# Block inverse of the delta rule: where the second orientation of the inverse comes from in levels 0 to 4

## The reference

```python
decay = jnp.exp(jnp.where(tril, gc[..., :, None] - gc[..., None, :], -jnp.inf))
a_mat = jnp.where(strict, jnp.einsum('bhncd,bhnsd->bhncs', kb, kc) * decay, 0.0)
rhs = jnp.concatenate([vb, kb * jnp.exp(gc)[..., None]], axis=-1)
sol = lax.linalg.triangular_solve(a_mat, rhs, left_side=True, lower=True, unit_diagonal=True)
...
v_new = u_c - jnp.einsum('bhcd,bhde->bhce', w_c, state)
```

## Time and profile before

| | |
|---|---|
| runs (3) | median 1034.73 us, 1033.13 to 1035.6 |
| profiled execution | 1033.16 us, its span 1031.4 us |
| mean granted TensorE clock | 0.939 of full speed |
| busy: PE, DVE, ACT | 859.6, 347.2, 216.8 us |
| the inverse in layer 0 | from about 95 to 144 us of the span |
| the inverse in layer 1 | from about 607 to 655 us |

### The profile page before, as it was taken

The page is one execution under the profiler, slowest core; times in us unless marked ns, Lnnn a source line. Parts: engine busy times, 40 slices in busy tenths (PEclk is TensorE's granted clock), DMA queues, the critical chain, the costliest instruction groups (busy, mean ns, idle before and its releaser), DMA issues.

```text
span 1031.4 us, 18112 instructions
## 1 busy us (share of the span) xinstructions
PE 859.6 (83%) x6932; PEld 617.0 (60%) x6933; DVE 347.2 (34%) x773; ACT 216.8 (21%) x410; POOL 23.0 (2%) x26
## 2 busy tenths in 40 slices
PE   4999999989588867698679999999896877879665
PEld 3877887968354433444358778879674544445332
DVE  1656634424621111111126565344346111111112
ACT  1243222222311100011103442133123111111111
POOL 1000000000300000000000000000003000000000
PEclk9999999989899888899879999999998998989888
DMA  9913012534459999979955120134344799899993
GB/s 343 350 57 103 1 42 82 167 119 163 169 244 419 421 420 421 421 323 421 403 207 183 42 82 1 45 119 163 107 172 157 306 420 421 337 423 419 420 421 138
DMA packets 48474, 249.42 MB, mean 242 GB/s; under 512 B 6096, under 2 KB 18560, under 8 KB 19344
## 3 DMA queue, kind: packets, MB, share of 16 engines
q1 hardware_dynamic: 47824, 246.91, 60.4%
q0 software_dynamic: 576, 1.43, 0.5%
HBM read 247.50 MB, written 1.05 MB: 241 GB/s over the span
## 4 chain that ended last, share of the span: by engine, by line
PE 50%; DMA 23%; DVE 12%; issue 7%; PEld 2%; ACT 2%; PEldq 1%; SPq 1%; DVEq 1%; POOLq 0%; ACTq 0%
PE ps L477 16%; DMA ring<-e_down 15%; PE ps L784 5%; PE ps L912 5%; PE ps L942 5%; DMA ring<-e_up 4%; PE ps L492 3%; PE ps L881 3%; DMA shared<-e_down 3%; DVE kq L1425 3%; DVE shared L1430 2%; PE ps L685 1%; PEld ps L912 1%; PE ps L639 1%; PE ps L953 1%
## 5 line engine op out<-in xcount | busy, mean ns | idle before, releaser
L477 PE MATMUL ps<-hT,ring 128*128 128x256 f32 x864 | 191.0, 381 | 0.0
L477 PEld LDWEIGHTS ps<-hT,ring 128*128 128x128 f32 x864 | 162.7, 190 | 25.9 <-issue 2.5
L912 PE MATMUL ps<-ring,hT 128*32 128x256 f32 x1728 | 114.7, 424 | 43.0 <-DMA ring<-e_up 21.7
L912 PEld LDWEIGHTS ps<-ring,hT 128*32 128x32 f32 x1728 | 67.2, 122 | 90.6 <-issue 69.8
L881 PEld LDWEIGHTS ps<-kq 128*128 128x128 bf16 x960 | 65.0, 149 | 10.0 <-issue 7.4
L953 PE MATMUL ps<-hT,kq 128*128 128x512 f32 x144 | 66.1, 602 | 5.5 <-PE ps L942 5.5
L881 PE MATMUL ps<-kq 128*128 128x128 bf16 x960 | 67.9, 235 | 2.3 <-DVE kq L1608 2.3
L1608 DVE TENSOR_TENSOR kq<-shapes,sel 128x128 bf16<-128x128 f32 (+1 forms) x40 | 9.9, 288 | 156.0 <-PE ps L920 155.7
L942 PE MATMUL ps<-ring,kq 128*32 128x512 f32 x448 | 51.0, 595 | 13.1 <-DMA ring<-e_down 8.4
L784 PE MATMUL ps<-ring,xn 128*128 128x256 f32 x256 | 58.8, 385 | 0.0
L912 PE MATMUL ps<-shared,hT 128*32 128x256 f32 x576 | 39.8, 437 | 21.9 <-DMA shared<-e_up 20.4
(11 more groups left out here) (303 smaller groups left out, 976.9 us busy)
## 6 DMA issues: line engine op xcount, KB each, us to landing
ring<-e_gate SPq DMA_DIRECT2D x48, 1024.0 KB, 21.8
ring<-e_up SPq DMA_DIRECT2D x48, 1024.0 KB, 10.8
ring<-e_down SPq DMA_DIRECT2D x48, 1024.0 KB, 23.6
ring<-w_mix SPq DMA_DIRECT2D x34, 1024.0 KB, 10.1
shared<-e_down SPq DMA_DIRECT2D x16, 1024.0 KB, 7.8
shared<-e_gate SPq DMA_DIRECT2D x16, 1024.0 KB, 18.7
shared<-e_up SPq DMA_DIRECT2D x16, 1024.0 KB, 26.5
ring<-w_mix SPq DMA_DIRECT2D x12, 512.0 KB, 7.2
```

Of the source, the lines that this page charges most:

```text
L477: mm = pe.matmul(bank[:, ct * T:(ct + 1) * T], w[:, k, ct * P:(ct + 1) * P], hT3[:, k, :], start=(k == 0), stop=(k == KD - 1))
L912: mm = pe.matmul(ps[32 * e:32 * e + 32, 5 + m, 0:DE], hq[:, k, 32 * e:32 * e + 32], slot[at[e]][:, k * DE:(k + 1) * DE], start=(k == 0), s ...
```

## The change

In levels 0 to 4 the non-zero blocks of XT are at most 32x32 and lie on the diagonal, so a transpose of each 32x32 block in its place is the transpose of the whole matrix. The changed kernel makes X so, with one VectorE instruction per group on 128x512 elements, from SBUF to SBUF. The TensorE transposes and the ScalarE copies stay for level 5 only. The SiLU on three gate tiles (L1076) now comes right after `gates(4)`, and 15 entries leave the list of banks.

```diff
-    order += [("A", g) for g in range(3)] + [("gate", 4)] + [("X", 0, g) for g in range(3)]
+    order += [("A", g) for g in range(3)] + [("gate", 4)]
     for lev in range(1, 7):
         order += [("W", lev, g) for g in range(3)] + [("Z", lev, g) for g in range(3)]
-        if lev < 6:
+        if lev == 5:
             order += [("X", lev, g) for g in range(3)]
...
-                for g in range(3):
-                    bank = begin(("X", 0, g))
-                    pe.wait_ge(xt_ready, g + 1)
-                    for m in range(4):
-                        mm = pe.transpose(bank[:, m * P:(m + 1) * P], XT[:, 4 * g + m, :], c("ident"))
-                    done(mm, ("X", 0, g))
...
-                    if lev < 6:
+                    if lev == 5:
                         for g in range(3):
                             bank = begin(("X", lev, g))
...
-                for lev in range(6):
-                    for g in range(3):
-                        bank = get(("X", lev, g))
-                        link(act.activation(X[:, 4 * g:4 * g + 4, :], bank[:, :], ACT.Copy))
-                        act.sem_inc(x_ready, 1)
-                        act.sem_inc(free[bank_of[("X", lev, g)][0]], 1)
-                    if lev == 0:
-                        act.activation(mixT[:, 2:5, :], mixT[:, 2:5, :], ACT.Silu).then_inc(gate_ready, 1)
+                act.activation(mixT[:, 2:5, :], mixT[:, 2:5, :], ACT.Silu).then_inc(gate_ready, 1)
+                for g in range(3):
+                    bank = get(("X", 5, g))
+                    link(act.activation(X[:, 4 * g:4 * g + 4, :], bank[:, :], ACT.Copy))
+                    act.sem_inc(x_ready, 1)
+                    act.sem_inc(free[bank_of[("X", 5, g)][0]], 1)
...
                     dve.sem_inc(xt_ready, 1)
+                    link(dve.transpose(X[:, 4 * g:4 * g + 4, :], XT[:, 4 * g:4 * g + 4, :]))
+                    dve.sem_inc(x_ready, 1)
...
                         free_(("Z", lev, g))
+                        if lev < 5:
+                            link(dve.transpose(X[:, 4 * g:4 * g + 4, :], XT[:, 4 * g:4 * g + 4, :]))
+                            dve.sem_inc(x_ready, 1)
```

## The result

The changed kernel takes 1041.37 us (median of 12 runs, 1037.3 to 1043.75), the kernel before 1035.13 in the same comparison (12 runs, 1032.65 to 1037.42). The ratio is 1.0061, with an interval of 1.0046 to 1.0075: slower by 6.2 us (4.8 to 7.8). The forecast was +8.3 us and 1043.0.

What follows compares the result with a forecast made beforehand. In the inverse, VectorE's linked chain of masks and subtractions plus a TensorE wait was taken as the path. Ten steps +10.0 and banks -1.7 gave +8.3 us: 1043.0 on the median of 1034.73, range 1038 to 1051.

Steps and rivals of the forecast that it cites:

- The wait of 1.76 goes, with a gain of 1.52 per step less what VectorE adds: Inverse, five steps per layer: masks' wait for TensorE falls from 1.76 to 0.24; net +1.00 us per step, +10.0 for ten.
- A transpose at 0.69: Inverse, VectorE: each of 15 transposes of 128x512 per layer takes 0.69 us, as L1412 does, with nothing covering it.
- rival C: Inverse, VectorE: transpose takes the fast single-source rate, 0.42 us; total +0.3 us, no slower. Chance 0.04.
- A: Inverse, VectorE: the transpose is slow, near 1.2 us; total +24.3 us, about 1059. Chance 0.08.
- Gaps of 0.15 behind a transpose: Inverse, VectorE: each transpose brings one gap of 0.15 us before the next instruction, bounds 0.04 and 0.24.
- The delay passes one to one: Behind the inverse: DMA queues are silent and wait for slots TensorE frees, so all later work moves with the delay.
- D: Whole kernel: the delay is swallowed later, or the inverse was not the bound; about 1033 to 1035 us. Chance 0.03.
- The clock stays at 1.00: Inverse, TensorE: at full clock its 5.7 us of a level's 8.7 do not become the bound.
- rival B: Inverse, TensorE: clock falls to half; a level costs 3.7 us more than now, about 1070 if it lasts. Chance 0.05.
- The bank side effect of -1.7: mLSTM output product ("o", 5): its turned bank is freed by the first L1507, not the second; 0.86 us saved per layer.

Runs made afterwards that it cites:

- experiment 3: Changed kernel without the VectorE transposes of levels 1 to 4, so the inverse is not computed: 1022.46 us, ratio 0.9880 to the kernel before.
- Experiment 7: Changed kernel with its VectorE transposes of levels 1 to 4 behind all three subtractions instead of behind each: 1043.75 us, ratio 1.0082 to the kernel before.
- experiment 2: Changed kernel with its list of banks turned back to the banks of the kernel before: 1043.12 us, ratio 1.0083 to the kernel before.
- experiment 1: Kernel before with only its list of banks turned by one, as the change turns it: 1029.95 us against 1035.20, ratio 0.9950.
- experiment 4: Kernel before with each W queued ahead of its group's transpose on TensorE and the Z's after: 1021.07 us, ratio 0.9862.
- experiment 6: Kernel before with W ahead of TensorE transposes, turned banks, and group 2's transposes of levels 0 to 4 on VectorE: 1019.96 us, ratio 0.9848.
- experiment 9: Kernel before with four unread TensorE products per layer in each of two mLSTM idle pieces: 1029.01 us against 1035.86, ratio 0.9942.
- experiment 10: Kernel before with each W ahead of its group's TensorE transpose and the list of banks turned by three: 1015.25 us, ratio 0.9806.
- experiment 11: The kernel of experiment 10 with four unread TensorE products per layer in the first mLSTM idle piece: 1014.87 us, ratio 0.9796 to the kernel before.
- experiment 8: Kernel before with four unread TensorE products per layer in the mLSTM's first idle piece of 2.37 us: 1034.72 us, ratio 0.9986.

## Why the forecast was right, and where a size was off

- *The wait of 1.76 goes, with a gain of 1.52 per step less what VectorE adds.* Right. The masks wait for TensorE no more, and a level was forecast at about 8.7 and is 8.75.
- *A transpose at 0.69.* It is 0.711, so the pass of one element per step of L1412 was the right row; 30 x 0.02 add 0.6. The inverses measure +10.4 for +10.0. This is also what the Vector Engine (DVE) Microarchitecture Reference of the Trainium skill, section 3.8, states for the transposing front end, one element per cycle per lane, and the trace agrees with its 711 ns against the 692 of L1412. The faster single-source pass of rival C (0.42) doesn't happen for it, so C falls; A (1.22) falls as well.
- *Gaps of 0.15 behind a transpose.* Right, 113.30 to 113.45.
- *The delay passes one to one.* Right: experiment 3 takes 18.9 away for 19.1 in its inverses and tails, and 60.4 us lie between inverse and tail in before and after alike. D falls.
- *The clock stays at 1.00.* Right for the inverse. Experiment 7 shows how near rival B stood: the same work in another order brings 0.81 over a level.
- *The bank side effect of -1.7.* Its mechanism was right (L679 starts behind the first reader and ahead of the second), and in the changed kernel its size was too: 1.4 by the tails, 1.75 by the medians (experiment 2). What the sum had at nothing is the clock behind the inverse. The tails gave -3.6, and the 2.2 beyond the banks come from where the low clock lies: before, it takes in the product of ("o", 5) and the work behind it, after, it is over ahead of that product. That is read from the traces; no run moves the fall alone. The forecast gave the clock a rival for the inverse (B) and none for the tail. The rows to see it were there: the earlier trace rows has 0.86 of waiting in layer 0, has 2.00 at the same place in layer 1, and the earlier trace rows has the 0.50 around the first. What a fall costs where no wait hides it is about 1.6 us per layer: experiment 1's tail is 2.5 shorter than before's, of which the bank gives 0.88, and filling both gaps with the old banks gives 1.6.

With +10.4 for +10.0 and -3.6 for -1.7 the forecast of 1043.0 becomes about 1041.5, and 1041.37 was measured. That the two agree to 0.2 is in part luck: the forecast stands on a median of three executions (1034.73), and the comparison had 1035.13 for the same kernel. Without the -2.2 of the clock, which the forecast did not have, the terms give about 1043.7, inside the range too.

Why did removing a wait of 1.52 ten times slow the kernel? The wait came from the order of TensorE's queue, W of group 0 behind all three groups' transposes, and not from the transposes' cost. Order alone takes it away (experiment 4: level 6.67, inverses 11.0 shorter, -14.1 us in all). The change took it away by moving 3 x 0.86 per level to VectorE, whose linked chain was the path: 8.75. What VectorE was given cost more than what it had waited for. VectorE: DVE Perf Modes of the Trainium skill, "Rules for kernel authors", calls that path the fastest for blocks of 32x32; per transpose the trace agrees (0.71 against 0.63 plus 0.60), and experiment 6 shows that the rule did not decide here.

Open are the first experts' loop of experiments 9 to 11, the -1.5 of experiment 8, and what decides whether the clock falls: behind the same idle piece of 2.37 ahead of the mLSTM it falls in some of these kernels and not in others (experiment 1).

## What to carry to other kernels

Before an engine's work is moved to take a wait away, look at what stands between the awaited instruction and its own inputs on its queue: if its inputs are ready and others' work is ahead of it, reorder first. Price the moved work on the queue that it goes to, at its full duration if that queue is a linked chain. And when a list of banks or buffers is edited, follow every fixed entry behind it: in the kernel before that side effect alone was worth 5.2 us, nearly as much as the change itself.

## What the runs showed of the hardware

- A transpose of 32x32 blocks on 128x512 float32 takes 711 ns on VectorE, 0.02 more than a two-source pass of that size.
- The same TensorE work in a level kept the clock at 1.00 with idle pieces of 0.66 to 0.81 and lost it (0.81 over the level, 0.50 for 3.4 us) with one piece of 2.53. Not every long piece brings a fall: behind the 2.37 of experiment 1 the clock stays at 1.00. TensorE: Matmul & The Clock Gate of the Trainium skill, Part 1, says that activity lifts the throttle and idleness brings it back; experiments 7 and 9 agree.
- With the same banks a tail takes 41.4 us without low clock (experiment 9), 41.9 and 42.1 with 3.4 us of it ahead of a wait for VectorE (experiment 2), and 43.1 with 3.4 us of it where TensorE runs on behind (before, layer 1): the low clock costs about 0.5 or about 1.6, by where it falls.
- Products that nobody reads made the kernel 0.6% faster where they filled two idle pieces of about 2 us (experiment 9), 3.3 of the 6.9 us shown in the tails. Where they filled one (experiment 8), the tails did not move.
